# Feed-forward of a decoder layer: where the later tokens are turned, in which order remainders are made, where a third weight pair lands, and when scaled sums are made

## What is computed

```
mix = concat(rwkv_out, mla_out) @ w_out
x   = LayerNorm(ALPHA * x + mix)
x   = LayerNorm(ALPHA * x + relu(x @ w_ffn1)^2 @ w_ffn2)
```

## Time and profile before

| what | value |
|---|---|
| median of 3 runs | 1488.87 us (1487.88 to 1488.96) |
| profiled execution, its own time | 1487.25 us |
| its span in the trace | 1485.5 us |
| TensorE busy | 1393.8 us, 94% of the span |
| VectorE busy | 919.2 us, 62% |
| ScalarE / GpSimd busy | 450.6 us, 30% / 466.2 us, 31% |
| mean granted TensorE clock | 0.968 of full speed |
| feed-forward 1 / 2 in the trace | about 833 to 1162 us / 1162 to 1485 us |

### The profile page before, as it was taken

One profiled execution on the slowest core, in us unless ns is written; L12 is line 12 of the kernel. 1 busy time (PEld: TensorE's weight loads), 2 busy tenths in 40 slices (PEclk: granted clock), 3 DMA queues, 4 the chain that ended last, 5 costly groups with the idle time before them and its releaser, 6 DMA issues.

```text
span 1485.5 us, 24855 instructions
## 1 busy us (share of the span) xinstructions
PE 1393.8 (94%) x10608; PEld 1145.3 (77%) x10608; DVE 919.2 (62%) x1017; ACT 450.6 (30%) x619; POOL 466.2 (31%) x285
## 2 busy tenths in 40 slices
PE   6999999888999879999599988999999999997997
PEld 5877888666777679996488866888888888886886
DVE  3547745264455334435738678777776786669687
ACT  2134533132443422332200442222221444332330
POOL 0000212110142100000107558666666264436030
PEclk8999999989999989999899999999999999998999
DMA  5111234587448942211051215444444987554653
GB/s 204 43 57 43 99 128 153 139 167 242 109 119 266 203 110 47 46 37 59 16 211 58 85 69 184 150 146 148 149 150 157 327 300 245 188 195 141 195 188 128
DMA packets 144686, 211.80 MB, mean 143 GB/s; under 512 B 79456, under 2 KB 82144, under 8 KB 143936
## 3 DMA queue, kind: packets, MB, share of 16 engines
q1 hardware_dynamic: 144384, 209.69, 44.6%
q10 hardware_dynamic: 192, 0.52, 0.1%
HBM read 136.18 MB, written 64.29 MB: 135 GB/s over the span
## 4 chain that ended last, share of the span: by engine, by line
PE 45%; DVE 3%; issue 1%; POOL 1%; DMA 0%; ACT 0%; SPq 0%; DVEq 0%; POOLq 0%
PE banks L2321 20%; PE banks L2243 18%; PE banks L2202 6%; PE banks L2231 1%; DVE x_out L2630 1%; DVE x_out L2633 0%; DMA w_landed<-in_w_ffn 0%; PE banks L2293 0%; PE banks L2209 0%; DVE t_lo L2531 0%; DVE stage_b_lo L2564 0%; DVE stage_a_lo L2561 0%; DVE x1T_lo L2531 0%; POOL tile_s L2739 0%; DVE u_all L2624 0%
## 5 line engine op out<-in xcount | busy, mean ns | idle before, releaser
L2321 PE MATMUL banks<-stage_b_hi,stage_a_hi 128*128 128x512 f32 x448 | 175.5, 392 | 8.5 <-DVE stage_b_lo L2564 8.5
L2321 PE MATMUL banks<-stage_b_lo,stage_a_hi 128*128 128x512 f32 x448 | 175.3, 391 | 0.0
L2321 PE MATMUL banks<-stage_b_hi,stage_a_lo 128*128 128x512 f32 x448 | 175.2, 391 | 0.0
L2561 DVE TENSOR_TENSOR stage_a_lo<-stage_a_raw,stage_a_hi 128x1024 fp32r<-128x1024 f32 x56 | 102.0, 1822 | 42.7 <-ACT stage_a_hi L2414 42.7
L358 PE MATMUL banks<-xT_hi,win_hi 128*128 128x512 f32 x320 | 103.4, 405 | 4.8 <-DVE xT_lo L705 4.8
L2321 PEld LDWEIGHTS banks<-stage_b_hi,stage_a_hi 128*128 128x128 f32 x448 | 84.8, 189 | 26.6 <-DVE stage_b_lo L2564 8.9
L358 PE MATMUL banks<-xT_lo,win_hi 128*128 128x512 f32 x320 | 100.3, 395 | 0.0
L358 PE MATMUL banks<-xT_hi,win_lo 128*128 128x512 f32 x320 | 99.6, 393 | 0.0
L2321 PEld LDWEIGHTS banks<-stage_b_lo,stage_a_hi 128*128 128x128 f32 x448 | 84.8, 189 | 17.7
L2321 PEld LDWEIGHTS banks<-stage_b_hi,stage_a_lo 128*128 128x128 f32 x448 | 84.7, 189 | 17.7
L2414 ACT ACTIVATE stage_a_hi<-stage_a_raw 128x1024 fp32r<-128x1024 f32 x56 | 59.3, 1058 | 112.0 <-DMA stage_b_raw<-in_w_ffn 91.6
(11 more groups left out here) (396 smaller groups left out, 3676.0 us busy)
## 6 DMA issues: line engine op xcount, KB each, us to landing
stage_b_raw<-in_w_ffn SPq DMA_DIRECT2D x50, 512.0 KB, 4.7
w_landed<-in_w_ffn SPq DMA_DIRECT2D x32, 512.0 KB, 5.2
hid_s<-tile_s SPq DMA_DIRECT2D x64, 256.0 KB, 4.1
stage_a_raw<-hid_s SPq DMA_DIRECT2D x32, 512.0 KB, 3.7
hid_h<-tile_h SPq DMA_DIRECT2D x48, 256.0 KB, 2.0
stage_a_raw<-hid_h SPq DMA_DIRECT2D x24, 512.0 KB, 3.8
win_raw<-in_w_in SPq DMA_DIRECT2D x20, 512.0 KB, 3.6
x_tok<-in_x SPq DMA_DIRECT2D x8, 512.0 KB, 6.9
```

Of the source, the lines that this page charges most:

```text
L2321: last = nc.tensor.matmul(ps[:, bank, :], s[a][:, j, tok], s[b][:, j, :], start=p == 0 and j == 0 and n == 0, stop=p == NP - 1 and j == 1 ...
L2561: V.tensor_tensor(s["a_lo"][:], s["a_raw"][:], s["a_hi"][:].bitcast(F32), ALU.subtract).then_inc(lo2, 1)
```

## The change

1. TensorE turns the first two kt of the later tokens between the two halves (`part` 0 and 1) of pair 0's products on the first tokens, instead of behind both.
2. VectorE makes the 16 remainders sum by sum (all kt of n = 3, then of 1, 2, 4) instead of 3, 1, 2 for each kt and 4 at the end; the wait for first_mm 4 stands ahead of all of them; and `w_low(2, 0)` follows them, ahead of the squares. ScalarE makes the high parts of n = 4 ahead of the last two ReLU tiles.
3. The third pair lands in buffers of its own (64 to 70 KB, where the normalised x lay, and 184 KB), in three transfers. Its load waits for the turning and for the stores of x, no longer for the remainders of n = 1; its weight sums wait for first_mm 4 and not for hid_done. Two ReLU tiles move to 70 and 72 KB (in `b12_raw`) and so wait for the remainders of n = 1. `load1(3)` gets the waits that `load1(2)` had.
4. The six scaled sums are made two by two behind `low2` of steps 36, 38 and 40 instead of all at step 34; `add(3)` stands behind `combine(39)`.

```diff
...
     landed = {kb: mem.at(f"w_landed{kb}", kb, [P, 2, KT, P]) for kb in (190, 46, 70)}
+    third = mem.at("w_third", 64, [P, 3, HK, P])
+    third_a22 = mem.at("w_third_a22", 184, [P, HK, P])
...
         i, h = int(name[1]) - 1, int(name[2]) - 1
+        if u == 2:
+            return (third_a22[:] if i and h else third[:, 2 * i + h, :, :]).rearrange("p k m -> p (k m)")
...
                      (S12_, None, 46, 54), (S34_, None, 50, 58))
-    wset = lambda u: (first_set, second_set)[u] if u < 2 else (even_set, odd_set)[u % 2]
+    third_set = pieces("2", (A12_, third[:, 0:2, :, :].rearrange("p c k m -> p c (k m)"), 190, 194),
+                       (("a22",), third_a22[:].rearrange("p (c k) m -> p c (k m)", c=1), 182, 184),
+                       (S12_, None, 198, 202), (S34_, None, 174, 178))
+    wset = lambda u: (first_set, second_set, third_set)[u] if u < 3 else (even_set, odd_set)[u % 2]
...
     b22_bank = lambda kt: 5 + 2 * (kt % 2)
-    first_relu = [mem.at(f"first_relu{i}", 174 + 2 * i, [P, HALF]) for i in range(4)]
+    first_relu = [mem.at(f"first_relu{i}", kb, [P, HALF]) for i, kb in enumerate((174, 176, 70, 72))]
+    landed_by = lambda u: 32 * (u + 1) + (16 if u >= 2 else 0)
...
     LAST = STEPS - 4
+    BASE_AT = (36, 38, 40)
+    ADD_AT = {40: 3, 50: 5}
...
             def load1(u):
+                if u == 2:
+                    sp.dma_start(third[:, 0:2, :, :].rearrange("p c k m -> p (c k) m"), t["w_ffn1"][u]).then_inc(w1_in, 16)
+                    sp.dma_start(third[:, 2, :, :], t["w_ffn1"][u + NU][:, 0:HK, :]).then_inc(w1_in, 16)
+                    sp.dma_start(third_a22[:], t["w_ffn1"][u + NU][:, HK:KT, :]).then_inc(w1_in, 16)
+                    return
...
             sp.wait_ge(sums_w, 4)
-            sp.wait_ge(t_split[1][1], T_ALL)
+            sp.wait_ge(b12_ready, HK)
+            sp.wait_ge(b22_ready, HK)
+            sp.wait_ge(x1_out, 16 * TT)
...
                 if u < NU - 2:
+                    if u == 1:
+                        sp.wait_ge(hid_done, 4)
+                        sp.wait_ge(t_split[1][1], T_ALL)
...
                         last.then_inc(first_mm, 1)
-            pe.wait_ge(mixed, TT)
-            pe.wait_ge(normed, TT - 1)
-            pe.wait_ge(last_normed, 1)
-            for kt in range(2):
-                turn_high(kt)
+                if not part:
+                    pe.wait_ge(mixed, TT)
+                    pe.wait_ge(normed, TT - 1)
+                    pe.wait_ge(last_normed, 1)
+                    for kt in range(2):
+                        turn_high(kt)
...
                 act.wait_ge(first_mm, i + 1)
+                if i >= 2:
+                    act.wait_ge(t_split[1][1], T_ALL)
...
                 high_t(2, kt)
+            act.wait_ge(first_mm, 4)
+            for kt in range(HK):
+                high_t(4, kt)
...
             first_part(3)
-            for kt in range(HK):
-                high_t(4, kt)
...
                 if nxt < NU:
-                    act.wait_ge(w1_in, 32 * (nxt + 1))
-                    if nxt == 2:
-                        act.wait_ge(hid_done, 4)
-                    else:
+                    act.wait_ge(w1_in, landed_by(nxt))
+                    if nxt > 2:
...
                     w_high(nxt, 2)
+                    if nxt == 2:
+                        act.wait_ge(hid_done, 4)
...
                 w_low(1, i)
-            for kt in range(HK):
-                for n in (3, 1, 2):
+            dve.wait_ge(first_mm, 4)
+            for n in (3, 1, 2, 4):
+                for kt in range(HK):
                     low_t(n, kt)
-            dve.wait_ge(first_mm, 4)
-            for kt in range(HK):
-                low_t(4, kt)
+            w_low(2, 0)
...
                 if nxt < NU:
-                    w_low(nxt, 0)
+                    if u > 1:
+                        w_low(nxt, 0)
+                    else:
+                        dve.wait_ge(sums_w, 5)
                     w_low(nxt, 1)
+                if u == 1:
+                    dve.wait_ge(sums_w, 8)
+                    dve.wait_ge(hid_done, 4)
...
                     dve.wait_ge(x_back, 16 * TT)
-                    dve.wait_ge(read2, 4)
-                    for cut in (HI, LO):
-                        for h in range(2):
-                            at = xo[:, 4 + 2 * h:6 + 2 * h, cut]
-                            V.scalar_tensor_tensor(at, at, ALPHA, u3_all[h][:], ALU.mult, ALU.add).then_inc(based, 1)
-                    for h in range(2):
-                        at = xo[:, 2 * h:2 * h + 2, LO]
-                        V.scalar_tensor_tensor(at, at, ALPHA, p1_all[:, 2 * h:2 * h + 2, :], ALU.mult, ALU.add).then_inc(based, 1)
...
+            def base(n):
+                dve.wait_ge(read2, 4)
+                for h in range(2):
+                    if n < 2:
+                        at, part = xo[:, 4 + 2 * h:6 + 2 * h, (HI, LO)[n]], u3_all[h][:]
+                    else:
+                        at, part = xo[:, 2 * h:2 * h + 2, LO], p1_all[:, 2 * h:2 * h + 2, :]
+                    V.scalar_tensor_tensor(at, at, ALPHA, part, ALU.mult, ALU.add).then_inc(based, 1)
...
                     read((q - LAG) // NP)
+                if q in BASE_AT:
+                    base(BASE_AT.index(q))
...
                 if u == 2:
-                    pool.wait_ge(hid_done, 4)
+                    pool.wait_ge(first_mm, 4)
...
                     pool.wait_ge(prod, 7 * (u - 2))
-                pool.wait_ge(w1_in, 32 * (u + 1))
+                pool.wait_ge(w1_in, landed_by(u))
...
                     combine(q)
-                if (q - LAG) % NP == NP - 1 and (q - LAG) // NP in (3, 5):
-                    add((q - LAG) // NP)
+                if q in ADD_AT:
+                    add(ADD_AT[q])
...
```

## The result

The changed kernel takes 1474.26 us in the median of 4 runs (1473.56 to 1476.92), the kernel before 1488.38 us beside it (4 runs); the ratio is 0.9905 with a 95% interval of 0.989 to 0.992. The prediction was 1475.2 us, with 1469.5 to 1480.5 as its range. The profiled execution took 1473.56 us with a span of 1471.8 us, against 1487.25 and 1485.5 us.

The account below looks back on a forecast made before the run. TensorE, busy 94% of the span, was taken as the bound, so only its idle and slow time could be won: 2.2 + 11.5 = 13.7 us off 1487.25 gives 1473.55, plus 1.62 for the median: 1475.2 us, range 1469.5 to 1480.5.

Parts of the forecast that it names:

- The scaled sums: Late stretch, steps 34 to 41: TensorE's stage wait of 8.66 us and 2.87 us of slow clock vanish, gain 11.5 us.
- The step that named what hides the work: Late stretch: the scaled sums are the same work, but 11 us and more of slack before TensorE needs the splits hide it.
- (b): Late stretch: splits of steps 36 to 39 slip, TensorE waits 3 us plus 2.87 us of clock; 1481 us, chance 0.08.
- (c): Late stretch: GpSimd runs beside VectorE throughout, splits and scaled sums take 3.37 us each; 1499 us, slower, chance 0.03.
- The turning: Between the halves of pair 0's products: a new 0.7 us wait, the 1.28 us wait gone; gain 1.0 us, at least 0.6.
- The remainders: Pair 1, VectorE: six collide with GpSimd, ten take 0.61 us; all done at 881.2, wait ahead of p7 4.1 us.
- The slow return: At p7 of pair 1: the slow clock after the wait would cost nothing, with 4.8 us available for its 2.72.
- Rival (a): Early stretch: VectorE and GpSimd collide less, remainders run free beside the weight sums; gain 11 + 11.5, to 1466 us, chance 0.10.
- Up to the hidden tile: From the remainders to p6 of pair 2: p6 at 897.0 instead of 899.15, gain 2.2 us including the turning's 1.0.
- w_low(2, 3) is in VectorE's way: Ahead of p6 of pair 2: after hidden sums end at 891.7, this split holds VectorE until 892.8.
- the early parts: Everything up to p6 of pair 2, turning included: gain 2.2 us, with 0.9 to 6 as the range.
- The sum: Whole kernel: 2.2 + 11.5 = 13.7 us gained, 1473.55 us for the profiled execution.

Follow-up runs that it names:

- E6: The changed kernel with all scaled sums and the addition back at step 34 as before; 1486.16 us, ratio 0.999.
- E7: The changed kernel with all six scaled sums at step 34 again, the addition left behind combine(39); 1474.03 us, ratio 0.991.
- E8: The changed kernel with the addition again ahead of combine(35) and the scaled sums two by two at steps 34, 36, 38; 1477.86 us, ratio 0.993.
- E3: The changed kernel with GpSimd's four weight sums of pair 2 held back until all 16 remainders are done; 1475.15 us, ratio 0.9909.
- E5: The kernel before with only the scaled sums spread behind steps 36, 38, 40 and the addition behind combine(39); 1476.1 us, ratio 0.9917.
- E2: The changed kernel with the remainders in the old order (n = 3, 1, 2 for each kt, then 4); 1473.75 us, ratio 0.9906.
- E9: The changed kernel with the banks of pair 2 handed out in another order; 1468.24 us, ratio 0.9865.
- E1: The changed kernel measured again, nothing altered; 1473.59 us, ratio 0.9899.
- E11: The changed kernel with all turning back behind both halves of pair 0's products; 1476.44 us, ratio 0.9922.
- E12: The changed kernel measured a third time, nothing altered; 1475.49 us, ratio 0.9914.
- E4: The changed kernel with w_low(2, 0) behind the four squares instead of ahead of them; 1473.59 us, ratio 0.9899.
- E10: The changed kernel with both E9's bank order and E4's squares ahead of w_low(2, 0); 1469.92 us, ratio 0.9879.

## Why the prediction was right, and where it was off

**The scaled sums**, 11.5 us predicted: 11.4 us (E6 against the changed kernel), with the granted clock at 1.00 from 1325 to 1366 us. The step that named what hides the work holds. What the prediction left open is which half of the edit does it. E7 and E8 answer: the addition's place alone is enough, and the spread sums alone give 8.6 of the 11.4 us. Rivals (b) and (c) fall, VectorE was always through with a step in time.

**The turning**, 1.0 us with 0.6 as the lower bound: the last matmul of p3 of pair 1 starts 867.17 - 832.30 = 34.87 us after pair 0's start instead of 868.17 - 832.74 = 35.43, so 0.56 us. This term was sized too high, and its lower bound too. The new wait was 0.88 us instead of 0.7, and the later one of 0.35 us did not shrink below 0.3.

**The remainders.** The count of collisions held: n = 3 ready at 871.4 (871.5 predicted), n = 1 at 876.0 (876.3), all at 880.8 (881.2), the wait ahead of p7 3.91 us (4.1). All 16 took 16.2 us with six collisions, so one took 1.7 us where 1.8 was counted. The slow return stretched p7 and cost nothing, as predicted. Rival (a), free-running remainders beside the weight sums, is refuted by these rows. E3 is no second test of it, since there the weight sums come later.

**Up to the hidden tile**, p6 at 897.0 predicted, 896.27 measured; from pair 0's start 64.3 and 64.0. The step "w_low(2, 3) is in VectorE's way" failed: VectorE won more hand-overs than counted, had `w_low(2, 2)` done at 887.2 instead of 890.3 and `w_low(2, 3)` at 889.4 instead of 892.8, and then waited 2.65 us for the hidden sums, which took 8.8 us instead of 8.2. So the one wait did not break into two, p5 did not wait at all, and the return cost 2.16 us where 1.61 was kept. That p6 came out within 0.3 us all the same is in part luck: measured from pair 0's start the hidden sums ended 0.7 us later than the prediction had them, and the 1.1 us of a split behind them fell away. In sum the early parts gave 1.5 to 1.9 us (E5, E6) where the term was 2.2.

**The sum**, 13.7 us predicted, was 13.3 us in the stretch that the change touches. That the two spans differ by exactly 13.7 us is luck of the start, and so is that the median came 0.9 us below the forecast.

Worth more than the early parts is what they did not touch: the wait at p6 did not give way to another order of the remainders (E2) or of the colliding work (E3), for it was a wait for a bank, and E9 got four to five times their gain from that.

## What to carry to other kernels

When a wait sits behind a chain of two engines that take turns at the same memory, reordering within the chain may only move the wait, as in E2 and E3; look first whether what the product waits for, here a bank, can be handed out differently (E9). Before work is spread over several steps, look at what stands behind it in another engine's list: moving one addition of GpSimd behind five combinations did all that the spreading of six VectorE instructions was there for (E7), and the spreading without it did three quarters (E8).

## What the runs showed of the hardware that was not expected

**Where the half clock falls counts as much as how long the wait was.** Behind a single wait of 5.5 to 6.0 us (nine profiles: before, changed, E1, E5, E6, E7, E8, E11, E12) the 1152 matmuls from p6 of pair 2 took 262.8 to 264.0 us, against 261.15 at the even pace; 6 to 12 matmuls start 0.43 us apart there, at a granted clock of 0.50, and their number differs between executions of the same kernel (9, 9 and 12 in changed, E1 and E12). Behind a wait of 1.04 us (E2) or 1.98 us (E4) they took 261.4 us. But two waits are not always cheaper than one: in E3 a wait of 4.84 us slowed all of p5, and one of 3.47 us behind it slowed seven more matmuls (262.96 us). Nor does the length of a wait decide alone: nine slow matmuls came behind the 2.28 us of E4, none behind the 2.29 us of E10. In E4 they stood ahead of another wait and so cost nothing.

**Taking turns is not the rule in both directions.** Beside GpSimd's instructions that follow each other, VectorE's remainders and GpSimd's sums alternate (1.7 us for each pair). But GpSimd's first weight sum of E3, which began at 880.83 us, 0.2 us after a VectorE split, lasted 4.56 us where it takes 1.29 alone: the split and the four squares went ahead of it without a gap. The Trainium skill says in SBUF — State Buffer, section Who interferes with whom, that whichever begins first gets the shared ports for its whole instruction and the other is blocked. In both cases one engine waits while the other works, which agrees. Which of the two goes next when both have work in their lists differs between the cases: in one they alternate (1.7 us for each pair), in the other VectorE's next instructions go ahead of a GpSimd instruction that waits already (4.56 us). The second is a reading of this one row, not shown further.
